# RWKV-7 layer of a two-layer backbone on one core: decay sums by a vector scan instead of triangular matmuls, with channels on partitions

## What is computed

```python
w_log = -softplus(-(w0 + tanh(xw @ w1) @ w2)) - 0.5        # per direction d, token t, channel c
a     = sigmoid(a0 + (xa @ a1) @ a2)
decay = exp(-exp(w_log))                                   # = exp(-e^-0.5 * sigmoid(w0 + ...))
...
S = S * w_t + sa * b_t + v_t * k_t                         # state, once per token, in each direction
```

## Time and profile before

| | us |
|---|---|
| median of 3 runs | 2400.82 (2397.12 to 2406.61) |
| profiled execution, its own time | 2408.59 |
| its span | 2406.8 |
| the 19 slots | from 1276 to about 1992 |
| TensorE busy over the span | 2235.9 (93%) |
| VectorE busy | 1054.1 (44%) |
| ScalarE busy | 893.5 (37%) |
| GpSimd busy | 707.1 (29%) |

### The profile page before, as it was taken

One profiled execution on the slowest core, in us unless ns is written; L12 is line 12 of the kernel. 1 busy time (PEld: TensorE's weight loads), 2 busy tenths in 40 slices (PEclk: granted clock), 3 DMA queues, 4 the chain that ended last, 5 costly groups with the idle time before them and its releaser, 6 DMA issues.

```text
span 2406.8 us, 63796 instructions
## 1 busy us (share of the span) xinstructions
PE 2235.9 (93%) x27583; PEld 1853.0 (77%) x27583; DVE 1054.1 (44%) x2108; ACT 893.5 (37%) x1707; POOL 707.1 (29%) x535
## 2 busy tenths in 40 slices
PE   5998999899999999989997898898889899999998
PEld 3775677788888888878875777777777768888887
DVE  3326666462111111176235566666666625311213
ACT  3435555333121212263223444554455323332333
POOL 0334455303323232203222313222231300344432
PEclk8999999999999999999998999999999979999999
DMA  8124555212122121213350000000000102323231
GB/s 258 53 53 142 177 173 180 66 53 70 54 69 70 53 70 53 70 36 111 104 160 21 3 25 24 24 4 24 25 12 17 40 20 77 99 88 105 87 103 55
DMA packets 172311, 176.30 MB, mean 73 GB/s; under 512 B 26512, under 2 KB 160032, under 8 KB 172064
## 3 DMA queue, kind: packets, MB, share of 16 engines
q1 hardware_dynamic: 171200, 169.48, 22.5%
q10 hardware_dynamic: 864, 3.15, 0.3%
HBM read 161.06 MB, written 11.53 MB: 72 GB/s over the span
## 4 chain that ended last, share of the span: by engine, by line
PE 83%; DVE 7%; ACT 4%; issue 3%; SPq 1%; DMA 1%; POOL 1%; ACTq 0%; DVEq 0%
PE PS L399 40%; PE PS L560 5%; PE PS L1530 5%; PE PS L419 4%; PE PS L1508 2%; PE PS L758 2%; PE PS L739 2%; PE PS L1314 2%; PE PS L1613 2%; PE PS L718 2%; PE PS L1518 2%; PE PS L1694 1%; PE PS L748 1%; PE PS L1125 1%; PE PS L1249 1%
## 5 line engine op out<-in xcount | busy, mean ns | idle before, releaser
L379 POOL TENSOR_TENSOR WL<-RAW,WH 128x1024 fp32r<-128x1024 f32 x160 | 383.6, 2420 | 940.5 <-ACT WH L360 940.5
L399 PE MATMUL PS<-AH,WH 128*128 128x256 f32 (+1 forms) x992 | 350.8, 354 | 3.3 <-DVE AL L2454 2.4
L399 PE MATMUL PS<-AH,WL 128*128 128x256 f32 (+1 forms) x992 | 351.7, 355 | 0.0
L399 PE MATMUL PS<-AL,WH 128*128 128x256 f32 (+1 forms) x992 | 349.1, 352 | 0.0
L360 ACT ACTIVATE WH<-RAW 128x1024 fp32r<-128x1024 f32 x160 | 159.9, 1048 | 273.3 <-PE PS L399 265.7
L399 PE MATMUL PS<-BH,WL 128*128 128x512 f32 (+1 forms) x672 | 239.2, 356 | 0.0
L399 PE MATMUL PS<-BH,WH 128*128 128x512 f32 (+1 forms) x672 | 238.5, 355 | 0.0
L399 PE MATMUL PS<-BL,WH 128*128 128x512 f32 (+1 forms) x672 | 237.6, 354 | 0.0
L399 PEld LDWEIGHTS PS<-AH,WH 128*128 128x128 f32 x992 | 187.8, 189 | 31.5 <-issue 2.6
L399 PEld LDWEIGHTS PS<-AL,WH 128*128 128x128 f32 x992 | 187.0, 188 | 27.1
L399 PEld LDWEIGHTS PS<-AH,WL 128*128 128x128 f32 x992 | 187.4, 189 | 25.3
(11 more groups left out here) (275 smaller groups left out, 4777.4 us busy)
## 6 DMA issues: line engine op xcount, KB each, us to landing
ADW<-l_ada_w SPq DMA_DIRECT2D x40, 1024.0 KB, 5.3
RAW<-l_mlp_up SPq DMA_DIRECT2D x64, 512.0 KB, 4.6
RAW<-l_mlp_down SPq DMA_DIRECT2D x64, 512.0 KB, 4.1
RAW<-l_w_rkv SPq DMA_DIRECT2D x24, 512.0 KB, 5.3
rwkv_scratch<-STG SPq DMA_DIRECT2D x24, 384.0 KB, 3.4
ADA<-l_ada_w SPq DMA_DIRECT2D x4, 2048.0 KB, 12.7
RAW<-l_w_in SPq DMA_DIRECT2D x16, 256.0 KB, 5.5
RAW<-l_w_out SPq DMA_DIRECT2D x16, 256.0 KB, 5.1
```

The lines of the kernel that those rows point to most:

```text
L379: e.tensor_tensor(WL[:, s, rows], RAW[:, s, rows], WH[:, s, rows], ALU.subtract).then_inc(w_split[h], 1)
L399: mm = e.matmul(dst, w[:, s, k, n * P:(n + 1) * P], r[:, k, lo:hi], start=(k == 0 and i == 0), stop=(k == KT - 1 and i == 2), skip_group_c ...
```

## The change

Weights now stand still and tokens move: z is made by two matmuls over 256 and 512 tokens with the 64 rows of `W2X` that belong to the direction, so that channels lie on partitions at once. The bias `w0`, halved, comes with the tanh. The sums over a chunk are made on VectorE, in place, by a scan `state = CARRY[t] * state + SG[t]`, where `CARRY` is 1 and, at each chunk's first token, 0; the backward direction reads and writes `SG` reversed. The exponentials read `SG` in SBUF. The triangular tables, the pads, the two tiles with a row of ones and four of six small loads per group are gone; one more row load (`w0`) stands in the list of loads at the start. Both order strings are new.

```diff
-        SLOT = (("pciipcpiicppcicpipipicicpipciipiipiipipciipic"
-                 "pipcpiicippciippiippcipipcpipippipiipicpiiii"),
-                ("ipcipiicpicppipppppiipipiicpiciipciipciipciipciip"
-                 "cicicpcpiicpcpicpicppipcpicippciciicppiciippciii"))
+        SLOT = (("ciicpipcipiciippcpipipcicpipcipiipipipicipicp"
+                 "ipiciipcipccpippicpipippipiipppiipiiippicii"),
+                ("iipcicppciiicppppcipciicpipicipcicipciipipciippii"
+                 "cpicpiicppicipicicppcpipipcpiipcicpiicippiciiipp"))
...
 def pe_pre(e, q):
-            for m in range(NTT):
-                mm = e.matmul(pair(3)[:, m * P:(m + 1) * P], LW[d][:, m * P:(m + 1) * P], W2X[:, d, :], start=True,
-                              stop=True, skip_group_check=True)
+            for a0, a1 in STREAMS:
+                mm = e.matmul(tile_ps(3)[:, a0:a1], W2X[HALVES[d], :], LW[HALVES[d], a0:a1], start=True, stop=True,
+                              skip_group_check=True)
             mm.then_inc(z_done, 1)
...
-                mm = e.matmul(tile_ps(3)[:, a0:a1], A2X[:, d, :], LA[:, a0:a1], start=True, stop=True, skip_group_check=True)
+                mm = e.matmul(tile_ps(3)[:, a0:a1], A2X[HALVES[d], :], LA[HALVES[d], a0:a1], start=True, stop=True, skip_group_check=True)
             mm.then_inc(a_done, 1)
             yield
             yield
-            e.wait_ge(a_tanh, q + 1)
-            e.wait_ge(sg_ready, q + 1)
-            for m in range(NTT):
-                mm = e.matmul(pair(3)[:, m * P:(m + 1) * P], SG[:, m, :], table(f"cum{d}"), start=True, stop=True,
-                              skip_group_check=True)
-            mm.then_inc(cum_done, 1)
             yield
             yield
             e.wait_ge(wi_ready, q + 1)
...
 def act_pre(e, q):
-            e.activation(SG[:, :, :].rearrange("p m c -> p (m c)"), pair(3)[:, 0:T], ACT.Tanh, scale=0.5).then_inc(sg_tanh, 1)
+            e.activation(SG[:, :], tile_ps(3), ACT.Tanh, bias=A0H[:, 16 + 8 * d + g:17 + 8 * d + g], scale=0.5).then_inc(sg_tanh, 1)
...
-            e.activation(wp_inclusive(w), chunks(pair(3)[:, 0:T]), ACT.Exp, scale=-DEC).then_inc(wp_ready, 1)
-            e.activation(WI[:, :], pair(3)[:, 0:T], ACT.Exp, scale=DEC).then_inc(wi_ready, 1)
+            e.activation(wp_inclusive(w), chunks(SG[:, :]), ACT.Exp, scale=-DEC).then_inc(wp_ready, 1)
+            e.activation(WI[:, :], SG[:, :], ACT.Exp, scale=DEC).then_inc(wi_ready, 1)
...
 def dve_pre(e, q):
-            e.tensor_scalar(SG[:, :, :], SG[:, :, :], 0.5, 0.5, ALU.mult, ALU.add).then_inc(sg_ready, 1)
+            e.tensor_scalar(SG[:, :], SG[:, :], 0.5, 0.5, ALU.mult, ALU.add).then_inc(sg_ready, 1)
+            e.wait_ge(sg_ready, q + 1)
+            sums = SG[:, ::-1] if d else SG[:, :]
+            e.tensor_tensor_scan(sums, CARRY[:, :], sums, 0.0, ALU.mult, ALU.add).then_inc(cum_done, 1)
...
 SyncE, per group
-                                 (W2X[0:64, 0, :], a["l1_w2"][0, :, cols]),
-                                 (W2X[64:128, 1, :], a["l1_w2"][1, :, cols]),
-                                 (W2X[64:65, 0, :], a["l1_w0"][0:1, cols]),
-                                 (W2X[0:1, 1, :], a["l1_w0"][1:2, cols]),
-                                 (A2X[0:64, 0, :], a["l1_a2"][0, :, cols]),
-                                 (A2X[64:128, 1, :], a["l1_a2"][1, :, cols])):
+                                 (W2X[:, :], a["l1_w2"].rearrange("d l c -> (d l) c")[:, cols]),
+                                 (A2X[:, :], a["l1_a2"].rearrange("d l c -> (d l) c")[:, cols])):
...
 ScalarE, before the slots
-            act.activation(LW[0][0:64, :], tile_ps(0)[0:64, :], ACT.Tanh)
-            act.activation(LW[1][64:128, :], tile_ps(0)[64:128, :], ACT.Tanh).then_inc(evac_act, 1)
+            act.activation(LW[:, :], tile_ps(0), ACT.Tanh).then_inc(evac_act, 1)
```

More of the change, by code:

```diff
@@ L94 @@
          "norm1_1": "l1_norm1", "norm2_1": "l1_norm2", "mu": "l1_mu", "k_k": "l1_k_k", "k_a": "l1_k_a",
-         "r_k": "l1_r_k", "ln_w": "l1_ln_w", "ln_b": "l1_ln_b", "final": "final_norm", "a0": "l1_a0"}
+         "r_k": "l1_r_k", "ln_w": "l1_ln_w", "ln_b": "l1_ln_b", "final": "final_norm", "a0": "l1_a0",
+         "w0": "l1_w0"}
 ROW_LOADS = len(PARAM) + 2 + 4
@@ L109 @@
 ROWS_A = {"ada_b0": 0, "ada_b1": 48, "norm1_0": 96, "norm2_0": 104, "norm1_1": 112, "norm2_1": 120}
-ROWS_B = {"mu": 0, "k_k": 48, "k_a": 56, "r_k": 64, "ln_w": 72, "ln_b": 80, "final": 88, "a0": 96}
+ROWS_B = {"mu": 0, "k_k": 48, "k_a": 56, "r_k": 64, "ln_w": 72, "ln_b": 80, "final": 88, "a0": 96, "w0": 112}
 ROWS_C = {"c": 0, "c_ctx": 8}
@@ L151, in build @@
         ONES = keep("ONES", [P, P])
-        A0H = keep("A0H", [P, 16])
         KA1 = keep("KA1", [P, KT])
         MU1, MU2 = PAR[:, 272:272 + KT], PAR[:, 280:280 + KT]
+        A0H = PAR[:, 128 + ROWS_B["a0"]:128 + ROWS_B["a0"] + 32]
         IDN, HEAD1, SWAP, SEL = CK[:, 0:128], CK[:, 128:256], CK[:, 256:384], CK[:, 384:386]
@@ L202, in build @@
         STG = place("STG", 102, [P, 4, T])
-        LW = [place("LW1", 120.25, [P, T]), place("LW0", 123.25, [P, T])][::-1]
+        LW = place("LW", 120.25, [P, T])
+        CARRY = place("CARRY", 123.25, [P, T])
         LA = place("LA", 126.25, [P, T])
@@ L221, in build @@
         WI = core("WI", [P, T])
-        SG = place("SG", core_at[0], [P, NTT, P])
+        SG = place("SG", core_at[0], [P, T])
         KB = core("KB", [P, NTT, 4, C])
@@ L227, in build @@
         CT = core("CT", [P, CORE_W])
-        W2X, A2X = core("W2X", [P, 2, P]), core("A2X", [P, 2, P])
+        W2X, A2X = core("W2X", [P, P]), core("A2X", [P, P])
         KG = core("KG", [P, T])
@@ L1158, in build @@
         NQ = 2 * KT
-        PADS = 10
+        PADS = 6
         def table(name):
@@ L1203, in build @@
         HALVES = (slice(0, 64), slice(64, 128))
-        SLOT = (("pciipcpiicppcicpipipicicpipciipiipiipipciipic"
-                 "pipcpiicippciippiippcipipcpipippipiipicpiiii"),
-                ("ipcipiicpicppipppppiipipiicpiciipciipciipciipciip"
-                 "cicicpcpiicpcpicpicppipcpicippciciicppiciippciii"))
+        SLOT = (("ciicpipcipiciippcpipipcicpipcipiipipipicipicp"
+                 "ipiciipcipccpippicpipippipiipppiipiiiippicii"),
+                ("iipcicppciiicppppcipciicpipicipcicipciipipciippii"
+                 "cpicpiicppicipicicppcpipipcpiipcicpiicippiciiipp"))
         def slots(e, pre, inverse, chain):
@@ L1220, in key_squares @@
         def key_squares(e, g):
-            e.wait_ge(ga_loaded, 112 * (g + 1) + 16)
+            e.wait_ge(ga_loaded, 48 * (g + 1) + 16)
             e.activation(TB[:, :], KG[:, :], ACT.Square, scale=col(1, ROWS_B["k_k"] + g)).then_inc(kk_sq, 1)
@@ L1863, in _ @@
                 v = a[PARAM[n]]
-                form = {"mu": "i (r c) -> (i r) c", "a0": "i (r c) -> (i r) c", "r_k": "(r h) c -> r (h c)"}
+                form = {"mu": "i (r c) -> (i r) c", "a0": "i (r c) -> (i r) c", "w0": "i (r c) -> (i r) c", "r_k": "(r h) c -> r (h c)"}
                 v = v.rearrange(form.get(n, "(r c) -> r c"), **({"h": 2} if n == "r_k" else {"c": P}))
@@ L2023, in _ @@
                     pool_split(pool, 2 * i + s, s)
-            for d in range(2):
-                pool.memset(LW[d][:, :], 0.0).then_inc(pads_ready, 1)
-            pool.wait_ge(pads_ready, 2)
+            pool.memset(CARRY[:, :], 1.0).then_inc(pads_ready, 1)
+            pool.wait_ge(pads_ready, 1)
+            pool.memset(CARRY[:, 0::C], 0.0).then_inc(pads_ready, 1)
             pool.wait_ge(w_split[1], U_LORA + 2)
-            pool.memset(LW[0][64:65, :], 1.0).then_inc(pads_ready, 1)
-            pool.memset(LW[1][0:1, :], 1.0).then_inc(pads_ready, 1)
             pool.wait_ge(w_used, U_LORA + 2)
-            pool.wait_ge(pads_ready, 4)
-            for w in (W2X, A2X):
-                pool.memset(w[:, :, :], 0.0).then_inc(pads_ready, 1)
             for b in range(2):
@@ L2226, in _ @@
             for b in range(3):
-                n = (P, 112, 16)[b]
+                n = (P, P, 16)[b]
                 pe.transpose(bank(7)[:, b * P:b * P + n], ROWS[0:n, b, :], IDN[0:n, 0:n]).then_inc(par_t, 1)
@@ L2400, in _ @@
             dve.wait_ge(par_t, 3)
-            dve.tensor_copy(PAR[:, 0:240], bank(7)[:, 0:240]).then_inc(par_ready, 1)
+            dve.tensor_copy(PAR[:, 0:256], bank(7)[:, 0:256]).then_inc(par_ready, 1)
             dve.tensor_copy(PAR[:, 256:272], bank(7)[:, 256:272]).then_inc(par_ready, 2)
@@ L2411, in _ @@
             dve.wait_ge(par_ready, 3)
-            dve.tensor_scalar(A0H[:, :], col(1, ROWS_B["a0"], 16), 0.5, None, ALU.mult).then_inc(consts1, 1)
+            dve.tensor_scalar(A0H[:, :], col(1, ROWS_B["a0"], 32), 0.5, None, ALU.mult).then_inc(consts1, 1)
             dve.tensor_scalar(MU1[:, :], col(1, 8 * 2, KT), -1.0, 1.0, ALU.mult, ALU.add).then_inc(par_ready, 1)
```

4 lines of the change are left out of this document (1 added, 3 removed).

## The result

| | before | changed |
|---|---|---|
| median, us | 2400.82 | 2414.95 (7 runs, 2405.9 to 2420.16) |
| ratio to before, 95% interval | | 1.0042 (1.0025 to 1.006) |
| profiled execution, us | 2408.59 | 2420.16 |
| TensorE's mean granted clock, whole span | 0.978 | 0.960 |
| TensorE busy, whole span, us | 2235.9 | 2245.0 |

The change made the kernel about 0.4% slower, where 0.9% less was forecast. TensorE's busy time was to fall by about 25 us and rose by 9. The profile of the changed kernel has two rows that the forecast had no place for. The first view is the busy time by stretch, over the slots and for slots 9, 10 and 11 (the columns are those of the earlier trace rows).

The account below looks back on a forecast made before the run. TensorE, busy 93% of the span, was taken as the bound. 23.3 us for the product + 1.6 for z's place - 2.4 idling - 0.3 at the start = 22.2 us off 2400.8, giving 2378.6 us, range 2364 to 2395.

Parts of the forecast that it names:

- That only 64 rows of the array are used I count at nothing: z by two matmuls on half the array's rows: 1.56 us against 1.58, the half-used array costing 0.
- I take the middle, 1.4 us: Length of each of 16 scans on VectorE, set between 0.95 and 1.9 us; 22 us of busy time.
- the upper end, 1.9: Longest scan on VectorE in its own case: two 0.95 us passes; 0.5 us late with a slow sigmoid.
- the slow rival: Scan on VectorE delays `WP`, `WI` and TensorE; gain used up at 3.0 us a scan, 2413 us at 3.8; chance 0.07.
- the prediction's own slopes: Gain against scan length: 22.2 us at 1.4, 16 us at 1.9, beyond that one-to-one delay, used up at 3.0.
- the prediction's estimate of about 1.8 us: Scan length on VectorE from the skill's half throughput applied to 0.95 us; sum 2 to 5 us smaller.
- It would idle there in any case: TensorE's hop behind the rate projection: 0.4 us stall inside 0.8 us idling, 0.34 more, 2.4 us over 7 even slots.
- The product's 23.3 us: Removing the triangular product from TensorE's path and the link to `WI` gains 15 x 1.55 us.
- z's place: z comes later in even slots, saving 0.23 us of TensorE idling ahead of it: 7 x 0.23 = 1.6 us gained.
- The first slot gives nothing: In the first slot VectorE runs without idling to `KB`, so TensorE's wait isn't for `WI`: no gain.
- VectorE taking the freed time: Rival: VectorE's pace behind `WI` eats two thirds of the product's gain, masks waited for longer; 2394.1 us; chance 0.17.
- `WI`'s waits did get smaller: TensorE's waits for `WI`: expected about unchanged; under 6 us meant wrong. Rival: two thirds go, 2366.6 us, chance 0.16.

Follow-up runs that it names:

- full_rows: The changed kernel with `W2X` and `A2X` zero-padded again, so z and the rate projection use all 128 array rows; 2397.98 us, ratio 0.9979 to the kernel before.
- rows_pool_waits: full_rows with GpSimd's six starting products of the inversion held back until the scan is through; 2389.56 us, ratio 0.9956 to the kernel before.

## Why the prediction was wrong

- **"That only 64 rows of the array are used I count at nothing"**: this step failed first. It is worth 15 us (9 to 22), by the granted clock. The matmul's duration at full clock was right (1.52 us for z where 1.56 were set), and it misled me: the price isn't in the instruction but in the speed of the 1.2 or 2.4 GHz stretches around it. The column with the granted clock stood in the earlier trace rows and I read it as a constant. No rival had a loss through the clock.
- **"I take the middle, 1.4 us"**: mis-sized. Alone the scan takes 1.76 us, beside GpSimd 2.16. Even the upper end, 1.9, was too low, though the hint stood in the earlier trace rows: the sigmoid's 0.55 or 1.11 us, which I used for the scan's own length only in the slow rival. By the prediction's own slopes (22.2 us gained at 1.4, 16 at 1.9, then 15 us for each microsecond) a scan of 2.16 us leaves 12 us, which makes the scan cost 12.5 us against 14.5 (8 to 21) measured. So the duration accounts for most of this miss. The Trainium skill (DVE: opcode table, instruction layouts, handler registers and perf-mode slots, section Datapath and trigger behaviour) gives such a scan half throughput; the prediction's estimate of about 1.8 us from it, which I set aside, agrees with the 1.76 us of the scan by itself.
- **"It would idle there in any case"**: charged at 2.4 us. With 2.16 us and a slow sigmoid the scan ends after the rate's tanh, so `WP` waits for it, and the hop's stall in slot 10 is 1.35 us instead of 0.4. In odd slots the wait for `WI` didn't absorb it either: in slot 11 TensorE waits 1.32 us for the update, and in all 15 hops 13.3 us. The sum was also a little kind here: with a sigmoid of 1.11 us and a scan of 1.4, sigmoid and scan end after 3.6 us, not 3.5.
- **The product's 23.3 us** fit the 20 us (13 to 27) that are left once both losses are out, against 22 to 25 us with z's place, and TensorE's busy time in full_rows is 24.5 us below the one before. But the 20 us hold the new order too, which by itself cost the kernel before 0.7%, so that the agreement is in part luck.
- **"The first slot gives nothing"** was right but for the clock: from z to the first products of the keys it took 11.1 us before and in full_rows, and 12.5 us in the changed kernel, where the rate projection ran at 1.2 GHz.
- **The rivals.** The slow scan had 0.07 and came nearest to what happened, with the wrong threshold: it was to decide from 3.0 us a scan, and 2.16 us took most of the gain. That its 2413 us are close to the 2415 measured is luck, for they stand on 3.8 us a scan and know nothing of the clock. VectorE taking the freed time was given 0.17; its sign, longer waits for the masks, didn't come (2.4 us of waits for `AR` against 7.1 before). `WI`'s waits did get smaller in the changed kernel (line 1673 waits 3.1 us for it), but the time went to the update's wait instead.
- **The two signs**: with the scan's price at 14.5 us the kernel would have been 0.2% faster, within what can't be told. Only with the rows' 15 us does it become slower.

What stays open is why matmuls over 64 rows lower the clock, and why the split scan and the moved piece of the odd string lower it as well. Of the 15 us and more that the split cost, the clock's part is seen in TensorE's busy time (8.6 and 10.8 us); the rest (longer total, an exponential that waits for the second half) wasn't run apart.

## What to carry to other kernels

Leaving out zero padding can cost more than it saves: try the full height of the array where TensorE also waits, as at the start of these slots, and read the granted clock of each version, and the busy time of the same instructions, before its durations are compared. When work moves from TensorE to VectorE, price it by the slow value beside GpSimd, and don't take idle time in the queue that it joins for free room while TensorE waits for that queue. If GpSimd has slack, a wait that keeps it quiet during VectorE's longest operation can be a cheap edit: here two lines gave about 0.2%.

## What the runs showed of the hardware

- Between executions of one kernel the time goes with the clock: the changed kernel took 2405.9 us at a mean granted clock of 0.965 and 2420.16 us at 0.960.
- Behind z on 64 rows the rate projection of slot 0 took 2.92 to 2.93 us at a granted clock that fell to 0.50, in five kernels; where both used 128 rows it took 1.56 us at 1.00, in eight.
- Same count, columns and place of the projections, 64 against 128 rows: granted clock 0.91 against 0.97 over the slots. With the rate projection alone changed, 0.96 against 0.98 in one execution each.
- A scan over 128x768 float32 with two inputs took 1.76 us alone and 2.16 us beside GpSimd's elementwise products; one over 128x384 took 0.94 to 0.96 us at its shortest and up to 1.36 and 1.41 us in other slots. In the backward direction, reading and writing reversed, it was no slower (1.757 to 1.759 us over all 16).
- `TENSOR_SCALAR` over 128x768 in SBUF took 0.55 us with GpSimd held back and up to 1.12 us in the changed kernel. It works the other way too: GpSimd's products, 0.72 us, took up to 2.06 us in the changed kernel and at most 1.12 us when they waited for the scan:

```profile
L1594 POOL TENSOR_TENSOR XIT<-MT_ALL,CT x96: 717/722/2062, 1306.2 to 1931.7; 64x256 f32<-64x256 f32 x96
```

```profile
L1596 POOL TENSOR_TENSOR XIT<-MT_ALL,CT x96: 720/726/1124, 1306.7 to 1903.6; 64x256 f32<-64x256 f32 x96
```

The first row is of the changed kernel, the second of rows_pool_waits.
- A tanh with a bias per partition took 0.90 us over 128x768 against 0.81 without; the exponentials took 0.85 and 0.83 us from SBUF against 0.81 and 0.80 from PSUM.
